# Layer norm beside the memory attention, one conv tile on TensorE, and an output projection begun with its ready half

## What is computed

```python
def conformer_conv(u, dw, dw_b, ln_g, ln_b):
    a, gate = jnp.split(u, 2, axis=-1)
    v = a * jax.nn.sigmoid(gate)                      # 768 channels
    v = lax.conv_general_dilated(v, dw[:, None, :], window_strides=(1,),
                                 padding=[(CONV_K - 1, 0)],            # 31 taps, depthwise
                                 dimension_numbers=('NWC', 'WIO', 'NWC'),
                                 feature_group_count=CONV_W) + dw_b
    return jax.nn.silu(layer_norm(v, ln_g, ln_b))

# layer 0
u = h @ a_w_in[i]
conv_out = conformer_conv(u[..., :2 * CONV_W] + a_b_glu[i], ...)
qm = rms_norm(u[..., 2 * CONV_W:].reshape(B, S, MEM_HEADS, HEAD_DIM), mem_q_norm_g[l])
mix = jnp.concatenate([conv_out, memory_attention(qm, mk, mv)], axis=-1)
x = x + mix @ w_out[l]

# second block
mix = jnp.concatenate([rms_norm_2(o_sb, g_grp_sb[i]), rms_norm_2(o_mla, g_grp_mla[i])], axis=-1) @ w_o[i]
x = x + rms_norm_2(mix, g_post_mix[i])
```

## Time and profile before

| what | value |
|---|---|
| median of three runs | 1187.19 us |
| the profiled execution | 1190.13 us |
| its span, first to last instruction | 1188.3 us |
| TensorE matmuls busy | 1082.7 us, 91% |
| VectorE busy | 781.2 us, 66% |
| ScalarE busy | 581.5 us, 49% |
| GpSimd busy | 184.7 us, 16% |
| mean granted TensorE clock | 0.905 |

### The profile page before, as it was taken

How to read it: one execution, slowest core, us unless ns; L and a number is a source line. 1 busy time by engine, 2 the same in 40 slices (tenths; PEclk the granted TensorE clock), 3 DMA queues, 4 the chain that set the end, 5 groups by cost and what they waited for, 6 DMA issues and landing times.

```text
span 1188.3 us, 18360 instructions
## 1 busy us (share of the span) xinstructions
PE 1082.7 (91%) x7222; PEld 981.0 (83%) x7222; DVE 781.2 (66%) x1507; ACT 581.5 (49%) x1062; POOL 184.7 (16%) x85
## 2 busy tenths in 40 slices
PE   5996699999999997998999999997889799999976
PEld 5995489899989986677988998995668799999865
DVE  4899785756678325575656647755464678777775
ACT  5542355444554323454554544545434465546454
POOL 1771011212211000000121221211000000000200
PEclk9996799999999865599999999996689899999978
DMA  8441034555544330001435545440031334454410
GB/s 335 178 144 69 1 142 145 190 180 196 180 177 176 110 149 32 1 1 38 175 143 213 179 176 212 176 150 4 1 142 54 125 143 178 178 213 161 176 54 36
DMA packets 22837, 158.33 MB, mean 133 GB/s; under 512 B 2528, under 2 KB 2784, under 8 KB 4448
## 3 DMA queue, kind: packets, MB, share of 16 engines
q1 hardware_dynamic: 21888, 153.51, 35.2%
q10 hardware_dynamic: 864, 3.65, 0.8%
HBM read 156.10 MB, written 1.05 MB: 132 GB/s over the span
## 4 chain that ended last, share of the span: by engine, by line
PE 67%; DVE 21%; ACT 7%; issue 3%; DMA 1%; POOL 0%; DVEq 0%; ACTq 0%
PE bank L665 63%; DVE obank L1740 5%; DVE split_lo L558 4%; PE obank L665 2%; ACT split_hi L550 2%; PE bank L795 1%; DVE square_sum L1732 1%; ACT hidden_parts L1234 1%; DVE hidden_parts L1732 1%; DVE x L1732 1%; ACT L1234 1%; DVE mlp_lo L1740 1%; DMA consts<-in_consts 1%; DVE tmp L1740 1%; ACT act_parts L1237 1%
## 5 line engine op out<-in xcount | busy, mean ns | idle before, releaser
L665 PE MATMUL bank<-act_parts,split_hi 128*128 128x256 f32 (+1 forms) x1632 | 334.3, 303 | 29.6 <-DVE split_lo L558 13.0
L558 DVE TENSOR_TENSOR split_lo<-ring,split_hi 128x1024 fp32r<-128x1024 f32 (+1 forms) x206 | 265.5, 1299 | 130.7 <-ACT split_hi L550 130.3
L550 ACT ACTIVATE split_hi<-ring 128x1024 fp32r<-128x1024 f32 (+1 forms) x280 | 287.8, 1045 | 114.1 <-PE bank L665 112.7
L558 POOL TENSOR_TENSOR split_lo<-ring,split_hi 128x1024 fp32r<-128x1024 f32 (+1 forms) x74 | 181.3, 2456 | 966.9 <-ACT split_hi L550 966.9
L665 PEld LDWEIGHTS bank<-act_parts,split_hi 128*128 128x128 f32 x1632 | 268.6, 199 | 41.0 <-issue 26.3
L665 PE MATMUL bank<-hidden_parts,split_hi 128*128 128x512 f32 (+1 forms) x816 | 265.5, 377 | 4.2 <-POOL split_lo L558 3.0
L665 PE MATMUL bank<-act_parts,split_lo 128*128 128x256 f32 x880 | 255.3, 290 | 0.0
L665 PE MATMUL bank<-hidden_parts,split_lo 128*128 128x256 f32 x752 | 210.2, 280 | 0.0
L665 PEld LDWEIGHTS bank<-hidden_parts,split_hi 128*128 128x128 f32 x816 | 148.7, 188 | 35.8 <-POOL split_lo L558 3.7
L665 PEld LDWEIGHTS bank<-act_parts,split_lo 128*128 128x128 f32 x880 | 175.9, 200 | 0.0
L665 PE MATMUL bank<-mlp_hi,split_hi 128*128 128x256 f32 x512 | 146.0, 285 | 4.6 <-POOL split_lo L558 2.3
(11 more groups left out here) (226 smaller groups left out, 1318.3 us busy)
## 6 DMA issues: line engine op xcount, KB each, us to landing
ring<-in_weights SPq DMA_DIRECT2D x141, 1024.0 KB, 4.8
ring<-in_weights SPq DMA_DIRECT2D x5, 768.0 KB, 4.1
x<-in_x ACTq DMA_DIRECT2D x1, 1024.0 KB, 7.7
y<-in_mem ACTq DMA_DIRECT2D x1, 1024.0 KB, 9.8
out<-x SPq DMA_DIRECT2D x4, 256.0 KB, 2.5
consts<-in_consts ACTq DMA_DIRECT2D x1, 867.5 KB, 12.9
ring<-in_weights SPq DMA_DIRECT2D x1, 512.0 KB, 3.7
consts<-in_consts ACTq DMA_DIRECT2D x1, 260.0 KB, 7.8
```

The source lines that it names most:

```text
L550: nc.scalar.activation(split_hi[:, w % SPLIT, 0:n], src, ACT.Copy).then_inc(sem("high_parts"), 1)
L558: (nc.vector if engine == "vector" else nc.gpsimd).tensor_tensor(split_lo[:, w % SPLIT, 0:n], src, split_hi[:, w % SPLIT, 0:n].bitcast(F32 ...
L665: return nc.tensor.matmul(dst, lhsT, rhs, start=start, stop=stop)
```

## The change

At the memory attention of layer 0:
- The sixth conv tile isn't done by VectorE. ScalarE writes, for each of its 31 taps, a 128x128 matrix with the tap's weights on the diagonal (`tap_diagonals`), in four portions between its work for mem_kv0 and mem_kv1. They lie where the high and low parts of the activations lie. TensorE sums 31 matmuls, diagonal by shifted input, into the tile `conv.sum`, right after the statistics of mk1; ScalarE adds the bias.
- VectorE does all remaining taps of the five other tiles, then the reciprocal for mk1 and `memory_keys(1)`, and only then the attention, without taps in its steps. TensorE's broadcast of mk1 stands between `conv.sum` and the attention.
- The sums of the mean stand after the scores of unit 1, those of the variance after the outputs of unit 0. VectorE centres the tiles in its step 1, ScalarE squares them before the exponentials of unit 2. The root, the reciprocal and the scaling follow the attention directly, ahead of the low parts of its output.
- The early load of the root's table on ScalarE and the eight dummy matmuls ahead of out0 are taken out, and the wait for the bf16 constants is moved to the second layer.

At o: after the MLA attention TensorE does k = 0 to 3 of tiles 0 and 1, then the transposes of the first token tile, k = 0 to 3 of tile 2, the transposes of the second, k = 0 to 3 of tile 3. The dummy matmuls are taken out. After `o.act` 2 it does k = 4 to 7 of these four tiles and then the other four tiles whole.

```diff
@@ psum_tiles
-    attention("mem0")
+    linear("conv.sum", 1)
+    linear("mk1.bc", 1)
+    out.extend(("mem0", "S", n) for n in range(2))
+    linear("ln.mean", 1)
+    out.extend([("mem0", "S", 2), ("mem0", "T", 0), ("mem0", "S", 3), ("mem0", "T", 1)])
+    linear("ln.var", 1)
+    out.extend(("mem0", "T", n) for n in range(2, 4))
     linear("mem0.oT", 2)
-    linear("mk1.bc", 1)
-    linear("ln.mean", 1)
-    linear("ln.var", 1)
...
@@ tensor
             head_stat("mk1", 4)
+            dst = take("conv.sum", 0)
+            pe.wait_ge(sem("glu.ready"), CONV_TILES)
+            for j in range(TAPS):
+                if j % 8 == 0:
+                    pe.wait_ge(sem("conv.diagonals"), min(TAPS, j + 8))
+                last = mm(dst[:, 0:SEQ], diagonals[:, j, :], glu[:, CONV_TILES - 1, j:j + SEQ], j == 0, j == TAPS - 1)
+            ready(last)
+            head_bcast("mk1")
...
-            attention("mem0")
+
+            def layer_norm_sums(w):
+                if w == 0:
+                    dst = take("ln.mean", 0)
+                    wait_emptied(pe, "conv.sum", 0)
+                    mm(dst[:, 0:SEQ], const("ones"), conv[:, CONV_TILES - 1, :], True, False)
+                    for c in range(CONV_TILES - 1):
+                        pe.wait_ge(sem("conv.done"), c + 1)
+                        last = mm(dst[:, 0:SEQ], const("ones"), conv[:, c, :], False, c == CONV_TILES - 2)
+                else:
+                    dst = take("ln.var", 0)
+                    for c in range(CONV_TILES):
+                        pe.wait_ge(sem("ln.squares"), c + 1)
+                        last = mm(dst[:, 0:SEQ], const("ones"), sq[:, c, :], c == 0, c == CONV_TILES - 1)
+                ready(last)
+
+            attention("mem0", layer_norm_sums)
...
-            pe.wait_ge(sem("bf16_consts"), 1)
-            keep_busy(take("out0", SPLIT), 8)
...
+            pe.wait_ge(sem("o.act"), 1)
+            for t in range(2):
+                take("o", t)
+                partial(t, 0, 4)
+            for t in range(2, SPLIT):
+                take("o", t)
             for tt in range(TT):
                 pe.wait_ge(sem("mla.o"), tt + 1)
                 dst = take("mla.oT", tt)
                 for i in range(4):
                     last = transpose(dst[:, 128 * i:128 * i + 128], otok[:, tt, 128 * i:128 * i + 128])
                 ready(last)
-            keep_busy(take("o", 0), 8)
+                partial(2 + tt, 0, 4)
             pe.wait_ge(sem("o.act"), 2)
-            linear("o", 0, KD, projected)
+            for t in range(SPLIT):
+                ready(partial(t, 4, KD))
+            linear("o", SPLIT, KD - SPLIT, projected)
@@ scalar
+            def tap_diagonals(first, end):
+
+                for j in range(first, end):
+                    do(diagonals[:, j, :], const("ident"), ACT.Copy, scale=const("dw", TAPS * (CONV_TILES - 1) + j, 1))\
+                        .then_inc(sem("conv.diagonals"), 1)
+
...
                     pump(f"mem_kv{l}", t)
+                    if l == 0:
+                        tap_diagonals(8 * t, 8 * t + 8)
...
                 if l == 0:
                     root("qm0", 8, 64)
+                    tap_diagonals(16, 24)
...
-            exponentials("mem0")
+            wait_tile(act, "conv.sum", 0)
+            do(conv[:, CONV_TILES - 1, :], bank("conv.sum", 0)[:, 0:SEQ], ACT.Identity, const("dw_b", CONV_TILES - 1, 1))\
+                .then_inc(emptied("conv.sum", 0), 1)
...
+            exponentials("mem0", layer_norm_squares)
...
-            load_root()
...
@@ vector
-            taps(12)
-            attention("mem0", finish_plain, lambda: taps(6))
+            taps(CONV_TILES * (TAPS + 1))
             invert("mk1", 8)
-            taps(10)
+            memory_keys(1)
...
+            attention("mem0", finish_plain, centre)
+            wait_emptied(dve, "ln.var", 0)
+            settle(nc.vector.reciprocal(tmp2[:, 0, 0:256], tmp[:, 0, 0:256]))
+            for c in range(CONV_TILES):
+                tt_(conv2[:, c, :], conv2[:, c, :], tmp2[:, 0, 0:256], ALU.mult).then_inc(sem("ln.scaled"), 1)
...
             mem_out("mem0")
-            memory_keys(1)
-            taps(CONV_TILES * (TAPS + 1))
```

More of the change, by code:

```diff
@@ L405, in build @@
         with nc.sbuf_tensor("sticks", [128, 8, 384], F32) as sticks:
+            pass
+        with nc.sbuf_tensor("diagonals", [128, 32, 128], F32) as diagonals:
             pass
@@ L846, in outputs, with attention @@
                     last.then_inc(sem("out_ready"), 1)
-            def attention(kind):
+            def attention(kind, beside=None):
                 units = UNITS[kind]
@@ L854, in attention @@
                         scores(kind, units[w + 1], w + 1)
+                    if beside is not None and w == 0:
+                        beside(w)
                     if 1 <= w <= len(units):
@@ L858, in attention @@
                         outputs(kind, units[w - 2], w - 2)
+                    if beside is not None and w == 2:
+                        beside(w)
             def group_scores(n):
@@ L982, in _ @@
             mem_out_transposed("mem0")
-            head_bcast("mk1")
             for tt in range(TT):
@@ L1195, in _, with partial @@
             attention("mla")
+            def partial(t, first, end):
+                w, _ = split_tile("o", t)
+                for k in range(first, end):
+                    last = product(bank("o", t)[:, 0:SEQ], [part[:, k, :] for part in w], [part[:, k, :] for part in projected],
+                                   k == 0, k == KD - 1)
+                return last
+            pe.wait_ge(sem("o.act"), 1)
[4 more added lines that the diff above has]
+                take("o", t)
             for tt in range(TT):
@@ L1280, in squares_of_x, with exponentials @@
                     pump(stage, first + t)
-            def exponentials(kind):
+            def exponentials(kind, between=None):
                 for n, u in enumerate(UNITS[kind]):
+                    if between is not None and n == 2:
+                        between()
                     slot = (FIRST_UNIT[kind] + n) % 2
@@ L1836, in attention @@
                     if between is not None:
-                        between()
+                        between(w)
                     if w >= 2 and units[w - 2].last:
@@ L1981, in _, with centre @@
             memory_keys(0)
-            taps(12)
-            attention("mem0", finish_plain, lambda: taps(6))
+            taps(CONV_TILES * (TAPS + 1))
             invert("mk1", 8)
-            taps(10)
+            memory_keys(1)
+            def centre(w):
+                if w == 1:
+                    dve.wait_ge(sem("conv.done"), CONV_TILES - 1)
+                    wait_emptied(dve, "conv.sum", 0)
+                    wait_tile(dve, "ln.mean", 0)
+                    for c in range(CONV_TILES):
+                        stt(conv2[:, c, :], bank("ln.mean", 0)[:, 0:SEQ], -1.0 / 768, conv[:, c, :], ALU.mult, ALU.add)\
+                            .then_inc(sem("ln.centered"), 1)
+                    dve.wait_ge(sem("ln.centered"), CONV_TILES)
+                    dve.sem_inc(emptied("ln.mean", 0), 1)
+            attention("mem0", finish_plain, centre)
+            wait_emptied(dve, "ln.var", 0)
+            settle(nc.vector.reciprocal(tmp2[:, 0, 0:256], tmp[:, 0, 0:256]))
+            for c in range(CONV_TILES):
+                tt_(conv2[:, c, :], conv2[:, c, :], tmp2[:, 0, 0:256], ALU.mult).then_inc(sem("ln.scaled"), 1)
             def mem_out(kind):
```

13 lines of the change are left out of this document (8 added, 5 removed).

## The result

The changed kernel takes 1179.31 us at the median of nine runs (1172.93 to 1181.98), the kernel before, run beside it, 1190.65 us (1183.33 to 1195.74). The ratio is 0.9904, 95% interval 0.9877 to 0.9932: faster by 11.4 us (8 to 15). The forecast, 13.0 us less, is a ratio of 0.9891.

What follows compares the result with a forecast made beforehand. TensorE was taken as the bound over most of the span, but not at layer 0's memory attention (VectorE's queue, then a chain of latencies) and the MLA attention's end. Gains 8.6 + 4.4 = 13.0 us gave 1174.2 us, range 1169 to 1184.

Steps and rivals of the forecast that it cites:

- Part 1: Memory attention of layer 0: 12.6 us of taps leave VectorE; TensorE's conv sum takes 14.3 us at the full clock.
- R1: Rival: the conv sum runs at the lower clock, scores start 9.4 us later, kernel at 1183.6 us; 7 in 100.
- Part 2: ScalarE's diagonals take 0.30 us each, so VectorE waits 1.4 us at the reciprocal for qm0.
- a sign of being right: TensorE idle for some 4 us before the mk1 broadcast.
- Part 3: All taps ahead of the attention end at 111.2; TensorE idles from 107.4 to about 111.5, broadcast of mk1 to 113.5.
- Part 4: Attention with layer norm inside, from 113.5: first out0 tile at 141.5 against 149.45, gain 7.9 us; 8.6 us taken.
- The term: Gain taken for the memory attention through out0: 8.6 us, with ends of 12 and about 3 us.
- Part 5: End of the MLA attention: o begins early and ends at 922.0 against 926.4, gain 4.4 us; ends 0 and 5.
- R2: Rival: o's early start gives nothing, as its input is later by what was moved; 1178.6 us; 12 in 100.
- R3: Rival: clock low from the conv sum to tile 0 of out0, 11 us slower, 1198.2 us; 5 in 100.
- R4: Rival: out0 starts earlier but nothing behind it, as later tiles wait for split weights; 1182.8 us; 7 in 100.

Runs made afterwards that it cites:

- o alone: The kernel before with only the change's lines of o, memory attention as before: 1182.28 us, ratio 0.9939 to the kernel before.
- attention part alone: The changed kernel with o as it was before, so only the memory attention's change: 1181.31 us, ratio 0.9916 to the kernel before.
- taps on VectorE: The changed kernel without diagonals and conv sum, VectorE doing the taps of all six tiles ahead of the attention: 1184.4 us, ratio 0.9969.
- 16 more: The changed kernel with 16 more fp32 matmuls of 256 columns on TensorE ahead of the conv sum: 1182.46 us in its one run.
- diagonals moved: The changed kernel with the diagonals written in other gaps of ScalarE, none ahead of qm0's root: 1172.43 us in its one run.
- low first: The changed kernel with VectorE forming the low parts of the attention's output before scaling the six tiles: 1171.61 us, ratio 0.9857 to the kernel before.
- old order: The kernel before with the sixth conv tile on TensorE, VectorE's order, layer norm and o as before: 1191.2 us, ratio 1.0025.
- all three: The changed kernel with diagonals moved, the attention's low parts first and five dummy matmuls in o's gap: 1170.77 us, ratio 0.985 to the kernel before.
- clock held: The kernel with all three edits plus ten dummy matmuls behind the transposes of the attention's output: 1172.81 us, ratio 0.9861 to the kernel before.

## Why the prediction was right, point by point

**Part 1, the price of the conv sum:** 14.3 us forecast, 13.63 measured at the full clock, 0.22 us a record, with each matmul's own stationary operand. R1 did not come.

**Part 2, the diagonals:** eight take 2.45 us, 0.30 us each; VectorE waited 1.25 us for 1.4. The estimate from rows holds. So does the one from the Trainium skill ("ScalarE: Activation LUTs", What ACT_TABLE_LOAD costs), 0.293 us each and 1.3 us of wait. What I missed is what that wait does to TensorE: it idled for 2.1 us, the clock fell about 1.4 us behind that (0.79 in the microsecond from 78), the projections behind ran slower and the conv sum began at 95.7, not 93.0. It cost nothing, as the broadcast waited for VectorE anyway (2.0 us instead of the 4.1 foreseen, which I had named as a sign of being right). The run with other places for the diagonals confirms that.

**Part 3, the order:** the taps end at 111.06, forecast 111.2. The new wait of TensorE is there. The two runs that separate order and taps show that my wording, 12.6 us "gone", was too simple: they are worth something only because the order changes too.

**Part 4, the chain:** the last outputs 126.7 to 128.7 (129.1), the out0 products at 134.06 (134.3), the first addition at 142.03 (141.5), the last at 160.05 (159.4). The granted clock fell in the microsecond from 112 (0.85), behind the broadcast, and not in the idle time ahead of it, so the sums of the mean took 3.87 us instead of 2.8 and the broadcast 1.09 instead of 1.98. That the two cancel is luck. At out0 the first of tile 0's half products still ran at the lower clock, so its six took 2.6 us and not 2.1. The first addition is 0.5 us later than forecast, or 1.0 us counted from the first statistics of each trace. The windows of the earlier trace rows place the old fall and rise at about 96.7 and 127.4, not at 96.8 and 127.2 as the prediction reads them; nothing hangs on it. The table loads stand back to back with their successors (125.76 + 1.28, then 127.06), as in the earlier trace rows, and the first Silu waits for VectorE. The drain that the Trainium skill states ("ScalarE: Activation LUTs", What ACT_TABLE_LOAD costs) isn't there. ScalarE's timeline of the kernel after:

```profile
125.76 1.28 ACT L1271 ACT_TABLE_LOAD   x1
127.06 0.47 ACT L1271 ACTIVATE tmp<-bank,consts 128x256 f32<-128x256 f32 x1
127.55 1.28 ACT L1271 ACT_TABLE_LOAD   x1
128.84 0.20 ACT L1271 ACTIVATE unused_roots<-consts 128x1 f32<-128x1 f32 x1
```

The term was 8.6 us. The profiled pair gives 7.8, counted from the first statistics of each. With the second trace of each kind (the run of o alone for the old code, 176.7, and the attention part alone, 169.6; both have their first statistics at 20.6) it is 7.5 us. So the term was about 1 us too large, and two traces of the same code differ by 2.3 and 3.0 us at this mark: the size is confirmed to no better than that.

**Part 5, o:** 4.4 us forecast. The profiled execution gave 3.0, because the clock fell at 894, behind a wait of 1.8 us, where I had reckoned with no fall. (The old chain from 901.4 ends at 904.5, not at 904.7 as the prediction adds up; that changes the term by 0.1 or 0.2 us.) But five of the six traces with the early start and no dummies there (o alone, taps on VectorE, 16 more, diagonals moved, low first) took 28.9 to 29.0 us, 4.4 to 4.5 less than before. The size was right; that the fall can happen was missing from the forecast's middle and stood only in its bounds. R2 is out.

**The sum:** 7.5 to 7.8 + 4.4 us is 11.9 to 12.2, and the ratio says 11.4 (8 to 15). The forecast's 13.0 lies inside, but with the smaller errors above pulling both ways. The 3.0 us more that the two profiles show arise in the NSA layer: over the eleven traces here that stretch, with the same instructions, takes from 207.2 to 214.5 us (213.9 before, 210.9 after), and the granted clock differs (0.78 before, 0.81 after, 0.82 in the shortest). The stretch from there to the last MLA outputs, untouched as well, takes from 316.9 to 324.1 us. It is not the change's. R3 and R4 did not come: out0's later tiles found their weights.

## What to carry to other kernels

Work that leaves a busy engine is worth nothing if the engine then waits for it: look at what is queued behind the new wait, and put that ahead. Of a chain that nothing hides, ask which result ends last before each engine's next step; one low part moved ahead of six scalings gave 2.0 us here, more than any attempt to keep the clock up. And don't read a difference of two or three microseconds out of one pair of traces: follow marks through the kernel, and see whether untouched stretches differ as much. Subtract what is there already at the first mark.

## What the runs showed of the hardware

The fall of TensorE's clock behind an idle time of a few microseconds is not repeatable. In o's gap of 1.77 us it fell in one of six executions. Behind the 2.1 us at qm0's broadcast it fell in four traces (after, 16 more, low first, old order), in the microseconds from 78 to 80, but not in the run of the attention part alone. Before the broadcast of mk1 it fell behind 2.00 us in the kernel after (0.85 in the microsecond from 112) and within the idle time in the four traces with some 4.9 us (attention part, diagonals moved, all three, clock held), but not behind 3.52 us in the run with the low parts first. Where the idle time was 1.8 to 2.1 us and the clock fell, TensorE was already busy again, for one to three microseconds. Where it is on the path, such a fall costs about 1.5 us here (30.4 instead of 28.9 to 29.0 us at o). It should be priced as a chance, not as none and not as certain. Dummy matmuls in a gap can move a fall to a worse place: 1.5 us lost in the last run.
